# Weight splits, residuals, PSUM opening and one SBUF address in a two-layer hybrid trunk on one core

## The reference

```python
for i in range(DEPTH):                                   # DEPTH = 2
    h = h + 0.5 * swiglu(rmsnorm(h, g_ffn1[i]), w1_ffn1[i], w3_ffn1[i], w2_ffn1[i])   # D_FF = 2816
    u = rmsnorm(h, g_mix[i])
    proj = u @ w_in[i]
    q, k, v, o_pre, i_pre, f_pre, z, xbc, dt_raw, gate_pre = jnp.split(proj, split_at, axis=-1)
    ha = mlstm_chunkwise(q, k, v, i_pre + b_igate[i], f_pre + b_fgate[i])
    ha = rmsnorm(ha, g_mlstm_head[i]) * jax.nn.sigmoid(o_pre)
    yb = ssd_chunked(xs, dt, a_neg, bm, cm)              # xs, bm, cm: xbc after a causal conv and silu
    yb = rmsnorm((yb + xs * d_skip[i]) * jax.nn.silu(z), g_ssm_out[i])
    g_a, g_b = jnp.split(jax.nn.sigmoid(gate_pre), N_BRANCH, axis=-1)
    merged = g_a * (ha @ w_branch_a[i]) + g_b * (yb @ w_branch_b[i])
    h = h + merged @ w_out[i]
    h = h + 0.5 * swiglu(rmsnorm(h, g_ffn2[i]), w1_ffn2[i], w3_ffn2[i], w2_ffn2[i])
    h = h + jax.nn.sigmoid(rmsnorm(h, g_ple[i]) @ w_ple_gate[i]) * (p[i] @ w_ple[i])
return rmsnorm(h, g_final)
```

## Time and profile before

| | us |
|---|---|
| median of 3 runs | 1630.81 |
| lowest and highest | 1628.36, 1634.38 |
| the profiled execution | 1634.04 |
| its span, first to last instruction | 1632.2 |
| PE busy | 1588.8 (97%) |
| PE loading weights | 1389.3 (85%) |
| DVE busy | 1047.6 (64%) |
| ACT busy | 730.7 (45%) |
| POOL busy | 213.5 (13%) |

### The profile page before, as it was taken

The page is one execution under the profiler, slowest core; times in us unless marked ns, Lnnn a source line. Parts: engine busy times, 40 slices in busy tenths (PEclk is TensorE's granted clock), DMA queues, the critical chain, the costliest instruction groups (busy, mean ns, idle before and its releaser), DMA issues.

```text
span 1632.2 us, 24437 instructions
## 1 busy us (share of the span) xinstructions
PE 1588.8 (97%) x9794; PEld 1389.3 (85%) x9794; DVE 1047.6 (64%) x1284; ACT 730.7 (45%) x882; POOL 213.5 (13%) x182
## 2 busy tenths in 40 slices
PE   7999989999999999999999999899999999999997
PEld 6888788999999978888778887888999999788885
DVE  5554578888877545554665555888887765555545
ACT  6344344434445345444554344344444534544444
POOL 1000013353330000000000000244344100000000
PEclk9999989999999999999999999999999999999999
DMA  8655534465545555555555554345544465466551
GB/s 252 195 180 186 174 104 130 130 172 140 151 129 181 204 162 190 197 180 188 164 183 186 185 183 147 109 129 152 166 146 129 155 200 188 143 204 197 182 181 65
DMA packets 245073, 270.85 MB, mean 166 GB/s; under 512 B 12560, under 2 KB 226152, under 8 KB 245012
## 3 DMA queue, kind: packets, MB, share of 16 engines
q1 hardware_dynamic: 239504, 266.90, 52.2%
q10 hardware_dynamic: 5364, 2.98, 0.7%
q0 software_dynamic: 144, 0.15, 0.0%
HBM read 268.94 MB, written 1.05 MB: 165 GB/s over the span
## 4 chain that ended last, share of the span: by engine, by line
PE 87%; DVE 7%; issue 3%; ACT 2%; POOL 1%; DMA 1%; SPq 0%; ACTq 0%; POOLq 0%; DVEq 0%
PE bank L1353 28%; PE bank L1379 16%; PE bank L1381 16%; PE bank L1380 16%; DVE xcv L1024 2%; DVE w_lo L814 2%; PE bank L1534 1%; PE bank L1423 1%; PE bank L1737 1%; PE bank L1596 1%; PE bank L1540 1%; ACT w_hi L518 1%; DVE xcv L1021 1%; PE bank L1374 1%; PE bank L1367 1%
## 5 line engine op out<-in xcount | busy, mean ns | idle before, releaser
L814 DVE TENSOR_TENSOR w_lo<-w_raw,w_hi 128x2048 fp32r<-128x2048 f32 x251 | 587.7, 2344 | 291.8 <-ACT w_hi L518 291.8
L518 ACT ACTIVATE w_hi<-w_raw 128x2048 fp32r<-128x2048 f32 x251 | 478.9, 1912 | 219.9 <-PE bank L1381 114.3
L1353 PE MATMUL bank<-u_hi,w_hi 128*128 128x256 f32 x1152 | 338.2, 294 | 2.5 <-DVE u_lo L849 2.5
L1353 PE MATMUL bank<-u_lo,w_hi 128*128 128x256 f32 x1152 | 324.3, 281 | 0.0
L1353 PE MATMUL bank<-u_hi,w_lo 128*128 128x256 f32 x1152 | 324.0, 281 | 0.0
L1379 PE MATMUL bank<-w_hi,ha_hi 128*128 128x512 f32 x704 | 280.2, 398 | 3.8 <-DVE w_lo L814 2.9
L1381 PE MATMUL bank<-w_hi,ha_lo 128*128 128x512 f32 x704 | 275.2, 391 | 0.0
L1380 PE MATMUL bank<-w_lo,ha_hi 128*128 128x512 f32 x704 | 274.6, 390 | 0.0
L1353 PEld LDWEIGHTS bank<-u_hi,w_hi 128*128 128x128 f32 x1152 | 221.6, 192 | 9.4 <-issue 8.6
L1353 PEld LDWEIGHTS bank<-u_lo,w_hi 128*128 128x128 f32 x1152 | 221.4, 192 | 5.1 <-issue 4.8
L1353 PEld LDWEIGHTS bank<-u_hi,w_lo 128*128 128x128 f32 x1152 | 221.3, 192 | 0.0
(11 more groups left out here) (272 smaller groups left out, 2359.5 us busy)
## 6 DMA issues: line engine op xcount, KB each, us to landing
w_raw<-in_w_ffn_dram SPq DMA_DIRECT2D x262, 512.0 KB, 4.4
w_raw<-in_w_in_dram SPq DMA_DIRECT2D x160, 512.0 KB, 4.8
w_raw<-in_w_branch_b_dram SPq DMA_DIRECT2D x32, 512.0 KB, 4.2
w_raw<-in_w_branch_a_dram SPq DMA_DIRECT2D x16, 512.0 KB, 4.5
w_raw<-in_w_out_dram SPq DMA_DIRECT2D x16, 512.0 KB, 4.1
w_raw<-in_w_ple_gate_dram SPq DMA_DIRECT2D x16, 512.0 KB, 4.6
y_feat<-in_w_ple_dram ACTq DMA_DIRECT2D x2, 1024.0 KB, 5.0
h<-in_x_dram SPq DMA_DIRECT2D x2, 512.0 KB, 5.3
```

Of the source, the lines that this page charges most:

```text
L518: a_.activation(whi[slot][:, :, :], raw[slot][:, :, :], ACT.Copy).then_inc(sem["w_hi"], 1)
L814: v_.tensor_tensor(wlo[slot][:, :, :], raw[slot][:, :, :], whi[slot][:, :, :].bitcast(F32), ALU.subtract).then_inc(sem["w_lo"], 1)
L1353: i = mm(o, w[slot][:, k, cs], x[:, k, :], start=(k + q == 0 and not seeded), stop=(k == KD - 1 and q == 2 and not seeded), skip_group_che ...
```

## The change

Five edits, in one:

- `yb_hi` and what lies behind it (`yb_lo`, `gate_b`, `mtmp`, `mrg`) move up by 768 bytes: y now begins at 512 modulo 1024, as u does. All other tiles stay where they are.
- In `residuals` at the mixer's entry (n = 1) all four h halves come first, then the 16 `low` steps.
- In PLE the split of K_PLE+3 comes ahead of the first tanh on ACT and of the first `gated` on DVE, in two halves with semaphores of their own; `variance` comes ahead of the split of K_PLE+2. PE starts the unit when the first half is there.
- The split of the next layer's unit 1 is in two halves too, in its old place.
- The four products with zeros in `ffn` are gone. The first down products of the first block (jj = 0, b = 0) open the banks with `start`; the first two blocks are written out and the loop starts at 1.

```diff
-        top[0] = place(top[0], 64)
+        top[0] = place(top[0], 320, 1024)
-        top[0] = place(top[0], 0)
+        top[0] = place(top[0], 512, 1024)
         u_hi = sb("u_hi", [P, KD, S], F32R)
-        a2 = place(base, 0)
+        a2 = place(base, 512, 1024)
         yb_hi, a2 = at("yb_hi", [P, SI // P, S], F32R, a2)
...
+            def shi_halves(lay, k):
+                slot = k % RING
+                act.wait_ge(w_raw[slot], (lay * (NU // RING) + k // RING + 1) * 32)
+                act.wait_ge(sem["unit_done"], lay * NU + k + 1)
+                for r, done in enumerate((sem["w_hi_half"], sem["w_hi"])):
+                    a_.activation(four(whi[slot])[:, 2 * r:2 * r + 2, :], four(raw[slot])[:, 2 * r:2 * r + 2, :],
+                                  ACT.Copy).then_inc(done, 1)
...
                 shi(lay, K_PLE + 2)
+                shi_halves(lay, K_PLE + 3)
                 act.wait_ge(sem["rms_ready"], lay * 4 + 4)
                 gate("gate_done", lay * 2 + 1, 0, 0)
-                shi(lay, K_PLE + 3)
...
-                    shi(lay + 1, 1)
+                    shi_halves(lay + 1, 1)
...
+            def slo_halves(lay, k, n):
+                slot = k % RING
+                for r, (before, after, v) in enumerate(((sem["w_hi_half"], sem["w_lo_half"], n),
+                                                        (sem["w_hi"], sem["w_lo"], lay * NU + k + 1))):
+                    dve.wait_ge(before, v)
+                    v_.tensor_tensor(four(wlo[slot])[:, 2 * r:2 * r + 2, :], four(raw[slot])[:, 2 * r:2 * r + 2, :],
+                                     four(whi[slot])[:, 2 * r:2 * r + 2, :].bitcast(F32), ALU.subtract).then_inc(after, 1)
...
+                joined(0)
                 if n == 1:
+                    joined(1)
+                    low(lay, n, 0, order)
+                    low(lay, n, 1, order)
                     weights()
...
+                variance(lay, 3)
                 slo(lay, K_PLE + 2)
-                variance(lay, 3)
+                slo_halves(lay, K_PLE + 3, lay * 2 + 1)
                 dve.wait_ge(sem["pp_ready"], lay * 4 + 4)
                 gated(lay * 4 + 1, 0, 0)
-                slo(lay, K_PLE + 3)
...
-                weights(lay, k0 + 1)
-                wide(s[1], 6, 0, x2, 4, False, True, ready=N * 16).then_inc(sem["up0_done"], 1)
+                if f == 0 and lay:
+                    pe.wait_ge(sem["w_lo_half"], lay * 2)
+                    wide(s[1], 6, 0, x2, 4, False, True, ready=N * 16,
+                         rest=lambda: weights(lay, k0 + 1)).then_inc(sem["up0_done"], 1)
...
-                for b in range(4):
-                    zero_bank(b)
...
-                                i = down(s[1], b, c, q)
+                                i = down(s[1], b, c, q, start=opens)
...
-                with nc.tensor.Fori(0, (FT - 3) // 2) as jj:
+                block(0, 0, True, opens=True)
+                block(0, 1, True)
+                with nc.tensor.Fori(1, (FT - 3) // 2) as jj:
...
-                weights(lay, K_PLE + 3)
-                wide(s[3], 1, 0, x2, 4, False, True).then_inc(sem["gate_done"], 1)
+                pe.wait_ge(sem["w_lo_half"], lay * 2 + 1)
+                wide(s[3], 1, 0, x2, 4, False, True, rest=lambda: weights(lay, K_PLE + 3)).then_inc(sem["gate_done"], 1)
```

More of the change, by code:

```diff
@@ L88, in sb, with place @@
             return t
-        def place(off, n):
-            return off + (n - off) % 256
-        top[0] = place(top[0], 64)
+        def place(off, n, period=256):
+            return off + (n - off) % period
+        top[0] = place(top[0], 320, 1024)
         raw = [sb(f"w_raw{i}", [P, KD, NP]) for i in range(RING)]
@@ L246, in trunk @@
         names = """up0_done h1T_done res_done uT_done gate_done y_out_ready rB_ready z_tanh o_tanh gate_tanh evac par_ready rdiag_ready rB_done ydiag_ready yB_done yB_ready wsm_hi_ready wsm_ready pre_row_ready pre_ready acs_exp cs_ready y_done ysum_ready
-            gtk_ready w_raw0 w_raw1 w_raw2 w_hi w_lo unit_done const_ready in_loaded0 in_loaded1 gains_loaded gains_tr par_taken w_first w_hi_first w_lo_first par_loaded
+            gtk_ready w_raw0 w_raw1 w_raw2 w_hi w_lo w_hi_half w_lo_half unit_done const_ready in_loaded0 in_loaded1 gains_loaded gains_tr par_taken w_first w_hi_first w_lo_first par_loaded
             wsm_loaded p_loaded out_stored rows_done m4_clear par_tr h_ready sq_ready var_ready rms_ready
@@ L858, in residuals, with joined @@
             def residuals(lay, n, stage, last, order, weights):
-                for c in range(NC):
+                def joined(c):
                     for q in range(2):
@@ L866, in residuals @@
                         residual(c, q)
-                    if c and n != 1:
-                        weights()
-                    low(lay, n, c, order)
+                joined(0)
                 if n == 1:
+                    joined(1)
+                    low(lay, n, 0, order)
+                    low(lay, n, 1, order)
                     weights()
+                else:
+                    low(lay, n, 0, order)
+                    joined(1)
+                    weights()
+                    low(lay, n, 1, order)
             def row_scale(lay, n):
@@ L1316, in _ @@
                 if lay + 1 < DEPTH:
-                    slo(lay + 1, 1)
+                    slo_halves(lay + 1, 1, lay * 2 + 2)
                     low(lay + 1, 0, 1, (4, 5, 0, 1))
@@ L1414, in ffn, with down @@
                 x2 = (U_HI[2 * f], U_LO[2 * f])
-                def down(slot, b, c, q, stop=False):
-                    return tall(slot, c, q, h1_hi[b], h1_lo[b], False, stop)
+                def down(slot, b, c, q, stop=False, start=False):
+                    return tall(slot, c, q, h1_hi[b], h1_lo[b], start, stop)
                 def h1_transposed(n, b):
@@ L1441, in ffn @@
                     i.then_inc(sem["par_tr"], 1)
-                weights(lay, k0 + 1)
-                wide(s[1], 6, 0, x2, 4, False, True, ready=N * 16).then_inc(sem["up0_done"], 1)
+                if f == 0 and lay:
+                    pe.wait_ge(sem["w_lo_half"], lay * 2)
+                    wide(s[1], 6, 0, x2, 4, False, True, ready=N * 16,
+                         rest=lambda: weights(lay, k0 + 1)).then_inc(sem["up0_done"], 1)
+                else:
+                    weights(lay, k0 + 1)
+                    wide(s[1], 6, 0, x2, 4, False, True, ready=N * 16).then_inc(sem["up0_done"], 1)
                 wide(s[0], 7, 1, x2, 0, True, False, ready=N * 16).then_inc(sem["unit_done"], 1)
@@ L1447, in ffn, with block @@
                     pe.wait_ge(sem["par_taken"], 1)
-                for b in range(4):
-                    zero_bank(b)
-                def block(jj, b, with_down):
+                def block(jj, b, with_down, opens=False):
                     j = jj * 2 + b
```

## The result

| | before | after |
|---|---|---|
| median, us | 1630.81 (1628.36 to 1634.38) | 1620.02 (1619.11 to 1621.21), 5 runs |
| profiled execution, us | 1634.04 | 1620.02 |
| its span, us | 1632.2 | 1618.3 |

The ratio of after to before is 0.9933, with a 95% interval of 0.9918 to 0.9949: 10.8 us less, and the interval stays clear of 1. The forecast was 1618.0 with a range of 1613.5 to 1624.5. The range held it and the sign was right. But the time lies between the forecast and rival (a), which was y at its slow pace and 1621.3, and the traces say that it is (a): y did not become faster.

A forecast was written before the change was run, and what follows sets the result against it. The prediction took PE's stream of matmuls as the bound (87% of the chain of waits). Its terms, 3.7 - 0.1 + 3.7 + 1.45 + 0.8 + 3.4 = 12.95 us, off the median 1630.81 gave 1618.0, range 1613.5 to 1624.5.

The forecast's parts named there:

- rival (a): Merge: y keeps the slow pace, as u does behind products with ones; 9.55 us won, 1621.3; chance 0.33.
- The bound: Whole kernel: PE is 87% of the chain of waits; only fewer matmuls, shorter PE waits or faster pace help.
- Down banks: Four FFNs: removing four products with zeros each saves 0.93 us a place, 3.7 us, less 0.1 for h1f in layer 1.
- PLE: Unit K_PLE+3 in each layer: earlier split in halves removes PE's wait for w_lo, 1.86 us each, together 3.7 us.
- Next layer's unit 1: Between the layers: w_lo in halves lets PE start at 821.8 instead of 823.29, 1.45 us, once.
- Mixer entry: Both layers: h halves first, transposes 0.65 us earlier, PE's weight matmuls 0.4 us; 0.8 us in all, bounds 0 and 1.3.
- y's address: Merge: y at 512 modulo 1024, like u, takes the fast 113 ns pace; 768 matmuls save 3.4 us.
- The clock: Mixer entry: half-clock stretch, about 2.7 us a layer, expected to stay; losing it or not moves time 3 us either way.
- (b): Layer's start or written-out blocks: waits give half back, 6 us or less won, 1625; chance 0.10.
- (c): Four FFNs: written-out blocks run dry in instruction fetch, slower, 1638; chance 0.04.
- (d): PLE: the wait for w_lo stays as the ring slot's release is elsewhere; 1622 with fast y; chance 0.03.

The follow-up runs named there:

- pace run: Microbenchmark, not the kernel: stretches of 48 fp32r 256-column matmuls, operand address raised by 64 bytes each, four entries ahead; 113.3 to 120.0 ns a matmul.

## Why the prediction was right, and where not

- **The bound.** Right. What the edits won is PE steps and PE waits that went; DVE and ACT keep their times (1047.0 and 731.1 us busy).
- **Down banks.** 3.7 foretold. 0.92 and 0.87 us at FFN 2 and 0.87 in layer 1's first FFN, by the run with the zeros back 0.87 to 0.96: about 3.6. The wait for h1f in layer 1 was foretold as 0.1 us, from a room of 2.5 us against 2.6 needed, and some 0.1 us is there.
- **PLE.** 3.7 foretold, 3.76 by its segments, 3.5 net. What the working missed is that PE, earlier by 1.86 us at the end of layer 0, loses 0.28 us of it there, in waits for h and for the next layer's w_lo half.
- **Next layer's unit 1.** 1.45 foretold, 1.47 by the undone edit.
- **Mixer entry.** 0.8 foretold, 1.2 measured, within its bounds of 0 to 1.3. The transposes are 0.64 us sooner, as foretold (0.65). The mis-sized term is what follows: I let whole durations follow one another (0.77 us to the end of h, then 2.16 of u_lo, then 0.35, and 0.1 to PE's start, which the text does not name). But successive steps on DVE overlap: the first u_lo starts 0.65 us after the down product's end, before h has ended, and the ninth 2.07 us after the first. PE starts 3.20 us after the down product's end where I had 3.37.
- **y's address.** This is the step that failed: "at the fast pace they save 3.4 us ... I take the fast one". Two things were wrong in it. I took the places modulo 1024, as the diff names them, and did not ask for the period. The pace run shows 256, and 512 and 768 are then one place. And I weighed u's starts behind any "other work" together, though y's starts have one thing ahead of them only, a product with zeros. The text had this as the case for rival (a), 0.33 for it; it should have been the forecast. With y at zero the sum is 9.55 and the time 1621.3. That the range held the time all the same was in part luck, as the next point says. The Trainium skill, "TensorE: Matmul & The Clock Gate" (Step-by-step: what each phase is for), says that the moving operand and the weight loads have read ports of their own. Read as "the distance changes nothing" it would have given the right sum here, and yet the runs show otherwise: 10.90, 11.31, 11.49 and 11.70 us for the same 96 matmuls.
- **What is left.** 1620.0 against 1621.3 of rival (a). The edits give 3.6 + 3.5 + 1.5 + 1.2 = 9.8 us, a quarter us over the sum without y, and the median fell by 10.8. Most of the last 1.0 us is the clock, by an estimate: 27 more executions of before that ran beside the experiments take 1636.4 and 1636.5 us at a mean granted clock of 0.988 and 1627.4 to 1628.9 at 0.996, and a line through all of them gives before 1630.3 us at 0.994. The five of after have a mean of 1620.2 us at a mean clock of 0.994. That is 10.1 us of difference, 0.3 over the edits' 9.8. So the forecast's distance of only 2.0 us owes 0.7 us to which executions of before were drawn and 0.4 to the mis-sized mixer term.
- **The clock.** That the low stretches stay at the entry, or are lost once, with 3 us either way, was right in kind: after has none at layer 0's entry and one of half the length at layer 1's. The price was set too high: 2.7 us for 6.8 at half clock, where the mixers' segments give 0.3 us for each us, 2.0.
- **Rivals (b), (c), (d).** The wait for u_lo stayed (2.5 and 2.6 us) and that for h1f grew by 0.1 us, no gap shows in the blocks written out, and the wait for w_lo in PLE is gone.

## What to carry to other kernels

Read a gain that rests on an address from at least two places that differ in the assumed way, and find the period first: one run of a microbenchmark would have shown that both places of this edit have the same pace. When an instruction is removed ahead of a long stretch of matmuls, count the pace of the stretch too: one product with zeros, 0.04 us by its step, cost 0.18 us at its successor and 0.4 us in the 95 matmuls behind it. And when several waits on one path are removed, set each against the next one as it will then stand; the second may be late by what the first gave.

## What the hardware showed that I had not expected

- 256-column fp32r matmuls at full clock run in steps of 113.3, 117.8, 118.7 or 120.0 ns by the place of the activations in SBUF modulo 256 bytes (with the weights at 64) and by what ran just ahead; the pace then holds for the whole stretch (144 matmuls at least). Only the distances 64 and 192 reach 113.3. In the mixer the same instructions at the same addresses took either pace from one execution to the next.
- The 512-column form, with the activations stationary, has 226.7 ns at distance 0, 233.3 at 64, 233.3 or 232.6 at 128 and 228.9 at 192 in the pace run: its best distance is the other form's worst. The FFN runs at the first (0.227 us) and PLE, whose u is at 192, at the last.
- A us at half the clock cost 0.3 us of time, not 0.5. PE is busy for 4.7 to 5.9 us of a low window of 6.8, so part of what it loses would have been waiting, as the wait of 0.5 us for `rdiag` that is missing behind a low entry. That this is the whole reason was not shown; in the two windows of 3.35 us PE is busy throughout.
